# One decoder step in hybrid layers: sums of squares moved to VectorE, nine stage barriers taken out

## The chip, the cores and the metric

The kernel runs on one NeuronCore of a Trainium2 chip. The metric is the device time of one execution in microseconds (us), the median of several runs. All data is fp32; matrix products are made of three fp32r products each, as told below.

## What is computed

One step of a decoder trunk of two layers, for a prompt of 512 tokens and 8 single sample tokens, side by side: 520 columns in all, `D_MODEL` 1024. Cut to what matters here:

```python
def rmsnorm(x, g):
    return x * rsqrt(mean(x * x, axis=-1) + EPS) * g

# layer 0: sliding-window attention and mLSTM; layer 1: Mamba-2 SSD and retention
x += mixer(rmsnorm(x, norm_mix) @ w_in) @ w_out
q, k, v = rmsnorm(x, norm_xattn) @ wq, rmsnorm(mem, norm_mem) @ wk, rmsnorm(mem, norm_mem) @ wv
x += softmax(norm(q) @ norm(k).T * s) @ v @ wo              # 4 heads, 256 memory tokens
x += square(relu(rmsnorm(x, norm_ffn) @ w1)) @ w2           # FFN_DIM 4096
```

Six of these norms are over `x`: before both input projections, both cross-attentions and both MLPs.

## The kernel before

Activations stand transposed: `x` is eight chunks `c` of 128 features (partitions) by 520 tokens (columns). A **norm** is never applied to its input. `NextNorm` (L277) makes three things from each chunk of `x` as soon as it is final: on VectorE `hi = x*g` rounded to fp32r (L290) and `lo = x*g - hi` (L291), on ScalarE the square (L297), which TensorE multiplies by a matrix of ones to sum it over the partitions into PSUM banks 6 and 7, chunk after chunk (L303, two halves of 260 columns, recorded as four matmuls). When all eight are summed, ScalarE makes `rstd` from it (L310, L312). The projection that follows works on `hi` and `lo`, and VectorE multiplies its result by `rstd` when it takes it out of PSUM.

**`Gemm`** (L320) runs a list of tiles. A tile is 128 output features by 520 columns over `nk` chunks of input features (8, or 4 in the cross-attention output and the odd output projection), and three matmuls for each chunk and half: hi by hi, hi weight by lo, lo weight by hi (L356 to L358). So a tile with `nk` 8 has 48 matmuls of 260 columns, one with 4 has 24. Tiles use three pairs of PSUM banks in turn; tile n waits until tile n-3 was taken out. The weights are streamed by SyncE through a ring of two buffers (L415): load of tile n+2 once the split of tile n is done, ScalarE's rounded copy `w_hi` (L399) once the load is there and tile n is computed, GpSimd's `w_lo = w - w_hi` (L410) after it, and then TensorE may begin. VectorE takes a tile out: `out_residual` adds it to `x` (L464), `out_ssd` multiplies by a per-token factor first and then adds (L2688, L2689), `out_copy` multiplies by `rstd` (L454). A tile with `"finish": c` makes chunk c of `x` final; after it `Gemm` calls the norm's steps: VectorE `NextNorm.dve`, ScalarE `NextNorm.act`, and TensorE `NextNorm.pe` one tile later, for the last chunk right at the end, and then ScalarE `act_rstd`. `follow` and `pe_before` hang other small steps on tiles; on each engine they stand in program order, and so does every wait.

**Stages** run one after another (`plan`, L2714), and between any two `fence` (L235) makes TensorE, VectorE and ScalarE drain and wait for each other; SyncE and GpSimd stream on. There are 41 such barriers. The order around the change is:

- `Load`: 8 chunks of the input transposed on TensorE, copied to `x` by VectorE, and the first norm; then the parameter vectors; barrier; even input projection.
- Mixer of the layer, of many small stages. The last but one of the even mixer is `MlstmSample`, of the odd one `SsdSample`, each followed by a norm stage; in the odd layer `OddStored` follows (ScalarE waits for stores).
- Output projection (even: 8 tiles of `nk` 8; odd: 16 tiles of `nk` 4, two for each chunk), with the norm of the cross-attention. Its first tile issues the load of the memory tokens (1 MB, ScalarE's queue). Barrier.
- `MemLoad` (L1585): the memory tokens transposed, split into hi and lo, in layer 0 also their norm. Barrier.
- Cross projection: 4 tiles `wq`, 4 `wk`, 4 `wv`; the last eight have 256 columns. `CrossNorm` (L1866) sums the squares of each q and k head on TensorE, in banks 6 and 7 too, before tile j+2.
- The attention over the memory, then the cross output projection: 8 tiles of `nk` 4, with the norm of the MLP. Barrier; in layer 0 `OddLoads` (two DMA issues) and a barrier.
- `Ffn` (L713): 64 tiles of `nk` 8; in layer 0 its last 8 finish `x` and make the odd mixer's norm. Barrier; `ConvHistory` (12 small transposes); barrier; odd input projection.

## Time and profile before

| | |
|---|---|
| median of 3 runs | 2122.76 us (2122.05 to 2124.38) |
| span of the profiled execution | 2111.2 us |
| its own time | not listed apart from its span; the median of the runs is 11.6 us above the span |
| TensorE, matmul busy | 1857.1 us, 88% |
| VectorE busy | 845.0 us, 40% |
| ScalarE busy | 585.5 us, 28% |
| GpSimd busy | 583.7 us, 28% |
| HBM | 80 GB/s over the span |

The profile is of one execution. Busy shares are of the span; "idle before" is the time an engine stood still ahead of an instruction, and what ended it. Times of stretches are counted from the start of the span. The matmul rows show a start and a modelled end that overlaps the next, so the pace of TensorE is read from start to start. The clock is what TensorE was granted, as a share of 2.4 GHz: 1.00 is that, 0.50 is 1.2 GHz.

### The profile page before, as it was taken

How to read it: one execution, taken by the hardware profiler on the slowest of the kernel's cores; microseconds unless marked ns; L12 is line 12 of the kernel's file. 1: busy time of each engine (PE TensorE's matmuls, PEld its weight loads, DVE VectorE, ACT ScalarE, POOL GpSimd, SP SyncE). 2: the span in 40 equal slices, each digit the busy share in tenths (PEclk: the TensorE clock that was granted, in tenths of full speed). 3: DMA queues.
4: the chain of work that ended last, by engine and by line, in shares of the span. 5: the costliest groups of instructions: out<-in, count | busy, mean ns of one | idle time of the engine just before them, and what ended most of it. 6: DMA issues, size and time to landing. Idle time of an engine off the chain costs nothing. (4 is left out here: it accounts for less than half of the span.)

```text
span 2111.2 us, 31312 instructions
## 1 busy us (share of the span) xinstructions
PE 1857.1 (88%) x13432; PEld 1700.7 (81%) x13432; DVE 845.0 (40%) x1201; ACT 585.5 (28%) x1006; POOL 583.7 (28%) x260
## 2 busy tenths in 40 slices
PE   7895777996999999999899978866986899999997
PEld 6894466885599999998899956745885489999997
DVE  4445265523332121234865244668733152111211
ACT  2234202242233232322331211325232233222311
POOL 1330000250134444442343300001331034444442
PEclk9997666997999999999999975678988999999999
DMA  4221001234033333332233213113226023333332
GB/s 116 71 80 43 20 23 55 66 100 179 21 105 98 92 91 90 93 89 62 80 91 86 75 49 93 27 40 114 87 70 219 1 71 90 93 96 93 90 91 81
DMA packets 294043, 170.64 MB, mean 81 GB/s; under 512 B 18839, under 2 KB 281159, under 8 KB 293754
## 3 DMA queue, kind: packets, MB, share of 16 engines
q1 hardware_dynamic: 253016, 123.85, 21.0%
q10 hardware_dynamic: 40890, 44.79, 6.5%
q8 instruction: 107, 1.75, 0.4%
q14 instruction: 30, 0.25, 0.0%
HBM read 155.91 MB, written 13.84 MB: 80 GB/s over the span
## 5 line engine op out<-in xcount | busy, mean ns | idle before, releaser
L410 POOL TENSOR_TENSOR w_lo<-w_raw,w_hi 128x1024 fp32r<-128x1024 f32 (+2 forms) x256 | 583.5, 2279 | 1502.7 <-ACT w_hi L399 1502.6
L356 PE MATMUL banks<-xn_hi,w_hi 128*128 128x260 f32 (+1 forms) x1920 | 552.4, 288 | 17.8 <-issue 11.1
L358 PE MATMUL banks<-xn_hi,w_lo 128*128 128x260 f32 (+1 forms) x1920 | 548.4, 286 | 0.0
L357 PE MATMUL banks<-xn_lo,w_hi 128*128 128x260 f32 (+1 forms) x1920 | 546.6, 285 | 0.0
L399 ACT ACTIVATE w_hi<-w_raw 128x1024 fp32r<-128x1024 f32 (+2 forms) x256 | 252.6, 988 | 1029.8 <-PE banks L358 997.2
L356 PEld LDWEIGHTS banks<-xn_hi,w_hi 128*128 128x128 f32 (+1 forms) x1920 | 364.0, 190 | 20.7 <-issue 18.2
L357 PEld LDWEIGHTS banks<-xn_lo,w_hi 128*128 128x128 f32 (+1 forms) x1920 | 363.6, 189 | 1.6
L358 PEld LDWEIGHTS banks<-xn_hi,w_lo 128*128 128x128 f32 (+1 forms) x1920 | 363.3, 189 | 1.1
L356 PE MATMUL banks<-hid_hi,w_hi 128*128 128x260 f32 x1024 | 290.3, 284 | 0.0
L358 PE MATMUL banks<-hid_hi,w_lo 128*128 128x260 f32 x1024 | 289.4, 283 | 0.0
L357 PE MATMUL banks<-hid_lo,w_hi 128*128 128x260 f32 x1024 | 288.6, 282 | 0.0
L464 DVE TENSOR_TENSOR x<-banks,x 128x520 f32<-128x520 f32 x96 | 67.1, 699 | 345.1 <-PE banks L358 345.1
L356 PEld LDWEIGHTS banks<-hid_hi,w_hi 128*128 128x128 f32 x1024 | 192.7, 188 | 0.2
L357 PEld LDWEIGHTS banks<-hid_lo,w_hi 128*128 128x128 f32 x1024 | 192.6, 188 | 0.2
L358 PEld LDWEIGHTS banks<-hid_hi,w_lo 128*128 128x128 f32 x1024 | 192.6, 188 | 0.0
L752 DVE SCALAR_TENSOR_TENSOR relu<-banks,rstd 128x520 f32<-128x520 f32 x64 | 44.8, 700 | 291.5 <-PE banks L358 291.5
L356 PE MATMUL banks<-y_hi,w_hi 128*128 128x260 f32 x320 | 97.3, 304 | 6.3 <-DVEq L237 4.3
L357 PE MATMUL banks<-y_lo,w_hi 128*128 128x260 f32 x320 | 93.3, 292 | 0.0
L358 PE MATMUL banks<-y_hi,w_lo 128*128 128x260 f32 x320 | 93.0, 291 | 0.0
L454 DVE TENSOR_TENSOR proj<-banks,rstd 128x520 f32<-128x520 f32 (+1 forms) x49 | 34.2, 698 | 145.4 <-PE banks L358 145.3
L356 PEld LDWEIGHTS banks<-y_hi,w_hi 128*128 128x128 f32 x320 | 63.3, 198 | 14.8 <-issue 9.7
L357 PEld LDWEIGHTS banks<-y_lo,w_hi 128*128 128x128 f32 x320 | 63.4, 198 | 0.4
(487 smaller groups left out, 2635.0 us busy)
## 6 DMA issues: line engine op xcount, KB each, us to landing
w_raw<-in_ffn_w SPq DMA_DIRECT2D x128, 512.0 KB, 4.0
w_raw<-in_odd_w_in SPq DMA_DIRECT2D x36, 512.0 KB, 3.8
kc<-in_cache_mem_k ACTq DMA_DIRECT2D x16, 512.0 KB, 7.5
vc<-in_cache_mem_v ACTq DMA_DIRECT2D x16, 512.0 KB, 11.5
w_raw<-in_even_w_in SPq DMA_DIRECT2D x14, 512.0 KB, 3.8
w_raw<-in_odd_w_out SPq DMA_DIRECT2D x24, 256.0 KB, 2.7
w_raw<-in_mem_wq SPq DMA_DIRECT2D x8, 512.0 KB, 3.8
w_raw<-in_mem_wk SPq DMA_DIRECT2D x8, 512.0 KB, 3.8
```

The lines of the kernel that those rows point to most:

```text
L356: pe.matmul(out, hi[:, kk, 0:m], r, start=kk == 0, stop=False)
L357: pe.matmul(out, hi[:, kk, 0:m], q, start=False, stop=False)
L358: last = pe.matmul(out, lo[:, kk, 0:m], r, start=False, stop=kk == nk - 1)
L399: act.activation(k.w_hi[n % RING][:, 0:t["nk"], 0:t["m"]], k.w_raw[n % RING][:, 0:t["nk"], 0:t["m"]], ACT.Copy).then_inc(k.w_hi_ready.s, 1)
L410: pool.tensor_tensor(k.w_lo[n % RING][:, view[0], view[1]], k.w_raw[n % RING][:, view[0], view[1]], k.w_hi[n % RING][:, view[0], view[1]]. ...
L454: dve.tensor_tensor(d, src, r, ALU.mult).then_inc(k.tile_out.s, 1)
L464: dve.tensor_tensor(d, src, d, ALU.add).then_inc(k.tile_out.s, 1)
L752: dve.scalar_tensor_tensor(two(self.relu[h % 2][:, :]), src, 0.0, two(k.rstd[:, :]), ALU.max, ALU.mult).then_inc(k.tile_out.s, 1)
```

## The change

It has four parts.

1. ScalarE makes `hi` (activation Copy with a scale) and the square of each chunk. VectorE makes `lo` and, from the second chunk on, adds the square to `norm_acc`. TensorE multiplies `norm_acc` by the ones once (`pe_total`), at the end of the first tile of the next projection (the tile marked `normed`), and `rstd` is made after that tile; VectorE waits for it before it takes that tile out.
2. A `normed` tile waits chunk by chunk for `lo` (`pe_chunk`), and stages marked `open_end` have no barrier behind them: `Load`, both cross output projections, `Ffn` of layer 0. `OddLoads`, `ConvHistory` and `OddStored` are no stages any more: their steps hang on the first tile of `Ffn`, on the third tile of the odd input projection (bank 6), and on the start of the second `MemLoad`.
3. Output projection and cross projection become one `Gemm` behind `MemLoad`: 4 tiles `wk`, the output tiles, 4 `wq`, 4 `wv`. So `MemLoad` comes ahead of the output projection, and the load of the memory tokens is issued at the start of `MlstmSample` and of `SsdSample`. In all nine barriers fewer.
4. On VectorE the norm's steps for chunk c come after the next tile was taken out. Counters of several helpers are shared so that the semaphores suffice.

```diff
-    def __init__(self, k, gain, dst, sq):
-        self.k, self.gain, self.dst, self.sq = k, gain, dst, sq
-        self.first = k.n_squares
-        k.n_squares += DC
+    def __init__(self, k, gain, dst, last_read=None):
+        self.k, self.gain, self.dst, self.last_read = k, gain, dst, last_read
+        self.nth = k.n_norms
+        k.n_norms += 1
+        self.first, self.adds = self.nth * DC, self.nth * (DC - 1)
+
+    def act(self, act, c):
+        k, x = self.k, self.k.x[:, c, :]
+        act.activation(self.dst[0][:, c, :], x, ACT.Copy, scale=k.col(self.gain + c)).then_inc(k.norm_high.s, 1)
+        if c >= 3:
+            act.wait_ge(k.square_added.s, self.adds + c - 2)
+        square = k.norm_sq[c % 2] if c else k.norm_acc
+        act.activation(square[:, :], x, ACT.Square).then_inc(k.square_ready.s, 1)
 
     def dve(self, dve, c):
-        k, x, g = self.k, self.k.x[:, c, :], self.k.col(self.gain + c)
-        hi, lo = self.dst[0][:, c, :], self.dst[1][:, c, :]
-        k.dve_link(dve.tensor_scalar(hi, x, g, None, ALU.mult))
-        dve.scalar_tensor_tensor(lo, x, g, hi.bitcast(F32), ALU.mult, ALU.subtract)
-
-    def act(self, act, c):
-        k = self.k
-        if c >= 2:
-            act.wait_ge(k.square_summed.s, self.first + c - 1)
-        act.activation(self.sq[c % 2][:, :], k.x[:, c, :], ACT.Square).then_inc(k.square_ready.s, 1)
-
-    def pe(self, pe, c):
-        k = self.k
-        pe.wait_ge(k.square_ready.s, self.first + c + 1)
+        k = self.k
+        dve.wait_ge(k.norm_high.s, self.first + c + 1)
+        dve.scalar_tensor_tensor(self.dst[1][:, c, :], k.x[:, c, :], k.col(self.gain + c),
+                                 self.dst[0][:, c, :].bitcast(F32), ALU.mult, ALU.subtract).then_inc(k.xn_ready.s, 1)
+        if c:
+            dve.wait_ge(k.square_ready.s, self.first + c + 1)
+            if c >= 2:
+                dve.wait_ge(k.square_added.s, self.adds + c - 1)
+            dve.tensor_tensor(k.norm_acc[:, :], k.norm_acc[:, :], k.norm_sq[c % 2][:, :], ALU.add)\
+               .then_inc(k.square_added.s, 1)
+
+    def pe_chunk(self, pe, c):
+        pe.wait_ge(self.k.xn_ready.s, self.first + c + 1)
+
+    def pe_total(self, pe):
+        k = self.k
+        pe.wait_ge(k.square_added.s, self.adds + DC - 1)
+        if self.last_read:
+            sig, count = self.last_read
+            pe.wait_ge(sig.s, count)
         for b, (c0, c1) in enumerate(HALVES):
-            last = pe.matmul(k.ps[:, 6 + b, 0:HALF], k.c("ones"), self.sq[c % 2][:, c0:c1],
-                             start=c == 0, stop=c == DC - 1)
+            last = pe.matmul(k.ps[:, 6 + b, 0:HALF], k.c("ones"), k.norm_acc[:, c0:c1], start=True, stop=True)
         last.then_inc(k.square_summed.s, 1)
 
     def act_rstd(self, act):
         k = self.k
-        act.wait_ge(k.square_summed.s, self.first + DC)
+        act.wait_ge(k.square_summed.s, self.nth + 1)
         k.act_link(act.activation(two(k.rstd[:, :]), k.ps[:, 6:8, 0:HALF], ACT.Ln, scale=1.0 / D_MODEL,
                                   bias=k.c("eps")))
-        act.activation(k.rstd[:, :], k.rstd[:, :], ACT.Exp, scale=-0.5)
-
-
-def next_norm(k, name, gain, dst):
-
-    return NextNorm(k, gain, dst, [k.small(f"{name}_sq{i}", [P, TOK]) for i in range(2)])
+        act.activation(k.rstd[:, :], k.rstd[:, :], ACT.Exp, scale=-0.5).then_inc(k.rstd_done.s, 1)
+
+    def rstd_here(self, eng):
+        eng.wait_ge(self.k.rstd_done.s, self.nth + 1)
...
-            if "pe_before" in t:
-                t["pe_before"](pe)
+            for step in t.get("pe_before", ()):
+                step(pe)
...
+                if "normed" in t:
+                    t["normed"].pe_chunk(pe, kk)
...
             last.then_inc(k.tile_done.s, 1)
-            if i and "finish" in self.mine[i - 1]:
-                self.norm.pe(pe, self.mine[i - 1]["finish"])
-        if "finish" in t:
-            self.norm.pe(pe, t["finish"])
+            if "normed" in t:
+                t["normed"].pe_total(pe)
...
+        late = None
         for i, t in enumerate(self.mine):
             n = self.base + i
+            if "normed" in t and late is not None:
+                self.norm.dve(dve, late)
+                late = None
             dve.wait_ge(k.tile_done.s, n + 1)
+            if "normed" in t:
+                t["normed"].rstd_here(dve)
             w = t["halves"][0][1] - t["halves"][0][0]
             nb = len(t["halves"])
             src = ps[0:t["m"], 2 * (n % 3):2 * (n % 3) + nb, 0:w]
...
             dve.wait_ge(k.tile_out.s, n + 1)
             for step in t.get("dve_after", ()):
                 step(dve, n)
-            if "finish" in t:
-                self.norm.dve(dve, t["finish"])
+            if late is not None:
+                self.norm.dve(dve, late)
+            late = t.get("finish")
+        if late is not None:
+            self.norm.dve(dve, late)
...
                 split_high(k, act, n + RING)
+            if "normed" in t:
+                t["normed"].act_rstd(act)
             if "finish" in t:
                 act.wait_ge(k.tile_out.s, n + 1)
                 self.norm.act(act, t["finish"])
             for step in t.get("act_after", ()):
                 step(act, n)
-        if "finish" in t:
-            self.norm.act_rstd(act)
...
-            if c:
-                self.norm.pe(pe, c - 1)
-        self.norm.pe(pe, DC - 1)
         pe.wait_ge(self.late_here.s, 16 * len(self.loads))
         pe.transpose(ps[:, 5, 0:self.n0], self.rows[0][0:self.n0, :], k.c("ident", self.n0)[:, 0:self.n0])
         pe.transpose(ps[:, 5, 128:182], self.rows[1][0:54, :], k.c("ident", 54)[:, 0:54]).then_inc(self.vectors.s, 1)
+        pe.wait_ge(self.out.s, DC)
+
+    def vectors_copied(self, pe):
+        pe.wait_ge(self.out.s, DC + 1)
...
-            dve.wait_ge(self.out.s, c + 1)
-            self.norm.dve(dve, c)
+            if c:
+                self.norm.dve(dve, c - 1)
+        self.norm.dve(dve, DC - 1)
         dve.wait_ge(self.vectors.s, 1)
...
+        tiles[0]["normed"] = normed
+        super().__init__(k, tiles, NextNorm(k, V_MIX + DC, k.xn) if layer == 0 else None)
...
+        prefetch_memory(k, act, self.mtok)
...
         k.state_stores_done()
         if l:
+            k.stores_done()
...
-    tiles = [gemm_tile(k.A["mem_wq"][l], [(h * P, P)], k.xc, out_copy(k, m.q[:, h, :])) for h in range(4)]
-    for w, dst in (("mem_wk", m.k_t), ("mem_wv", m.v_t)):
-        tiles += [gemm_tile(k.A[w][l], [(h * P, P)], (m.hm_hi, m.hm_lo), out_copy(k, dst[:, h, :]), halves=[(0, MEM)])
-                  for h in range(4)]
-    CrossNorm(k, tiles, [(m.q[:, h, :], V_QN + l) for h in range(4)] + [(m.k_t[:, h, :], V_KN + l) for h in range(4)], l)
-    s.append(Gemm(k, tiles))
+    memory_tiles = lambda w, dst: [gemm_tile(k.A[w][l], [(h * P, P)], (m.hm_hi, m.hm_lo), out_copy(k, dst[:, h, :]),
+                                             halves=[(0, MEM)]) for h in range(4)]
+    tiles = memory_tiles("mem_wk", m.k_t) + out_tiles
+    first = len(tiles)
+    tiles += [gemm_tile(k.A["mem_wq"][l], [(h * P, P)], k.xc, out_copy(k, m.q[:, h, :])) for h in range(4)]
+    tiles += memory_tiles("mem_wv", m.v_t)
+    k.small.reset(2080)
+    buffers = [k.small(f"qk_{n}{l}", [P, TOK]) for n in ("sq", "rstd0", "rstd1")]
+    keys = CrossNorm(k, tiles, 0, [(m.k_t[:, h, :], V_KN + l) for h in range(4)], buffers)
+    norm = NextNorm(k, V_XATT + DC * l, k.xc, (keys.rstd_ready, keys.base + 4))
+    tiles[first]["normed"] = norm
+    CrossNorm(k, tiles, first, [(m.q[:, h, :], V_QN + l) for h in range(4)], buffers, norm)
+    s.append(Gemm(k, tiles, norm))
     s += [KvTurn(k, m, l), CrossPrompt(k, m, l), CrossSample(k, m, l)]
     w = k.A["mem_wo"][l]
-    k.small.reset()
+    norm = NextNorm(k, V_FFN + DC * l, k.xn)
     s.append(Gemm(k, [gemm_tile(w, [(c * P, P)], (k.xa_hi, k.xa_lo), out_residual(k, c), nk=4, finish=c)
-                      for c in range(DC)], next_norm(k, f"cross_out{l}", V_FFN + DC * l, k.xn)))
-    return s
...
+    history = ConvHistory(k, normed)
+    gates, conv = OddGates(k), Conv(k, history)
+    follow(tiles, 2, lambda dve, n: history.dve(dve), pe=history.pe)
...
 def plan(k):
 
     stages = [Load(k)]
+    normed = stages[0].norm
     for layer, mixer in enumerate((even_layer, odd_layer)):
-        stages += mixer(k) + cross_layer(k, layer)
+        mixed, out_tiles = mixer(k, normed)
+        crossed, normed = cross_layer(k, layer, out_tiles)
+        ffn = Ffn(k, layer, normed)
         if layer == 0:
-            stages.append(OddLoads(k))
-        stages.append(Ffn(k, layer))
+            odd_loads(k, ffn.mine)
+            ffn.open_end = True
+        normed = ffn.norm
+        stages += mixed + crossed + [ffn]
...
                 s.pe(pe)
-                k.fence(pe, "pe")
+                if not s.open_end:
+                    k.fence(pe, "pe")
```

## Rows read from the trace of the kernel before

**Rows 1.** the page: busy time, share of the span and instructions of each engine

```profile
PE 1857.1 (88%) x13432; PEld 1700.7 (81%) x13432; DVE 845.0 (40%) x1201; ACT 585.5 (28%) x1006; POOL 583.7 (28%) x260
```

**Rows 2.** windows: bounds, length, busy by engine (instructions), clock, DMA share, GB/s

```profile
349.89:405.67 55.78, 54.94 (x416) 53.28 (x416) 30.92 (x24) 12.70 (x17) 18.44 (x8) 0.97 0.29 86
416.40:470.66 54.26, 51.90 (x408) 49.71 (x408) 10.79 (x19) 22.59 (x35) 25.69 (x11) 1.00 0.30 88
562.28:593.71 31.43, 30.62 (x224) 28.99 (x224) 24.17 (x24) 10.81 (x16) 11.79 (x8) 1.00 0.29 81
596.61:605.20 8.59, 8.59 (x51) 8.59 (x52) 0.03 (x1) 0.00 (x0) 0.00 (x0) 0.69 0.55 201
978.26:989.00 10.74, 10.74 (x68) 8.24 (x69) 1.98 (x3) 1.15 (x2) 0.85 (x1) 0.72 0.05 16
1469.82:1530.67 60.85, 55.74 (x416) 52.61 (x416) 44.45 (x47) 15.27 (x24) 23.27 (x16) 1.00 0.31 96
1690.98:1723.88 32.90, 32.09 (x224) 30.46 (x224) 24.04 (x24) 10.69 (x16) 11.89 (x8) 0.95 0.28 78
1725.51:1733.00 7.49, 7.49 (x52) 7.49 (x53) 0.07 (x1) 0.01 (x1) 0.00 (x0) 0.81 0.27 70
1730.00:1800.00 70.00, 70.00 (x588) 70.00 (x587) 16.09 (x23) 25.39 (x36) 30.56 (x12) 1.00 0.30 84
```

**Rows 3.** timeline, TensorE, one sum of squares between two tiles; start, us, instruction

```profile
362.80 1.04 PE L303 MATMUL banks<-even_out_sq,const 128*128 128x260 f32 x4
...
363.80 0.28 PE L357 MATMUL banks<-y_lo,w_hi 128*128 128x260 f32 x1
```

**Rows 4.** waits: total us, times, longest; even, then odd output projection

```profile
PE banks L303 <- ACT even_out_sq L297: 0.8, 1, 0.8
...
PE banks L303 <- ACT odd_out_sq L297: 5.1, 8, 2.3
```

**Rows 5.** timeline, TensorE: first matmul after six of the barriers [idle before it]

```profile
32.58 0.40 PE L356 MATMUL banks<-xn_hi,w_hi 128*36 128x260 f32 x1 [1.36 <-ACTq L237]
407.29 0.57 PE L1624 MATMUL banks<-const,mem_tok 128*128 128x128 f32 x2 [1.67 <-ACTq L237]
596.61 0.56 PE L356 MATMUL banks<-xn_hi,w_hi 128*128 128x260 f32 x1 [2.90 <-ACTq L237]
976.62 0.33 PE L679 MATMUL banks<-const,conv_old 24*128 24x24 f32 x3 [1.67 <-ACTq L237]
978.26 0.38 PE L356 MATMUL banks<-xn_hi,w_hi 128*16 128x260 f32 x1 [0.74 <-DVEq L237]
1725.51 0.56 PE L356 MATMUL banks<-xn_hi,w_hi 128*128 128x260 f32 x1 [1.63 <-DVEq L237]
```

**Rows 6.** weight split by shape, whole kernel: count, busy us, mean ns, idle before

```profile
L399 ACT ACTIVATE w_hi<-w_raw 128x512 fp32r<-128x512 f32 x40 | 25.1, 628 | 142.4 <-PE banks L358 134.2 <-DMA w_raw<-in_mem_wo 8.1
...
L410 POOL TENSOR_TENSOR w_lo<-w_raw,w_hi 128x1024 fp32r<-128x1024 f32 x214 | 530.2, 2478 | 978.9 <-ACT w_hi L399 978.8
L410 POOL TENSOR_TENSOR w_lo<-w_raw,w_hi 128x512 fp32r<-128x512 f32 x40 | 52.0, 1301 | 508.6 <-ACT w_hi L399 508.6
```

**Rows 7.** DMA issues: KB each, median us from issue to landing

```profile
w_raw<-in_ffn_w SPq DMA_DIRECT2D x128, 512.0 KB, 4.0
...
w_raw<-in_mem_wo SPq DMA_DIRECT2D x16, 256.0 KB, 2.7
```

**Rows 8.** VectorE by line, duration ns least/median/most

```profile
L2689 DVE TENSOR_TENSOR x<-x,odd_out_t x16: 699/1447/2678, 1473.8 to 1528.0; 128x520 f32<-128x520 f32 x16
...
L291 DVE SCALAR_TENSOR_TENSOR xc_lo<-x,vcol,xc_hi x16: 758/1768/2883, 358.6 to 1531.3; 128x520 fp32r<-128x520 f32 x16
...
L464 DVE TENSOR_TENSOR x<-banks,x x96: 684/700/701, 357.3 to 2094.6; 128x520 f32<-128x520 f32 x96
```

**Rows 9.** timeline, odd output projection: an add of VectorE and GpSimd beside it

```profile
1491.32 1.76 DVE L2689 TENSOR_TENSOR x<-x,odd_out_t 128x520 f32<-128x520 f32 x1
...
1491.23 1.30 POOL L410 TENSOR_TENSOR w_lo<-w_raw,w_hi 128x512 fp32r<-128x512 f32 x1 [2.92 <-ACT w_hi L399]
```

More of the change, by code:

```diff
@@ L465, in out_residual, with follow @@
     return emit
-def follow(tiles, i, dve=None, act=None):
-    for key, step in (("dve_after", dve), ("act_after", act)):
+def follow(tiles, i, dve=None, act=None, pe=None):
+    for key, step in (("dve_after", dve), ("act_after", act), ("pe_before", pe)):
         if step:
@@ L678, in pe @@
                 rows, n = src.shape
-                last = pe.transpose(k.ps[0:n, 4 + i % 4, c0:c0 + rows], src, self.ident(src, rows))
+                last = pe.transpose(k.ps[0:n, self.bank + i % 4, c0:c0 + rows], src, self.ident(src, rows))
             last.then_inc(self.done.s, 1)
@@ L756, in dve @@
             dve.wait_ge(k.tile_out.s, n + 1)
-            if "finish" in t:
-                self.norm.dve(dve, t["finish"])
+            if late is not None:
+                self.norm.dve(dve, late)
+            late = t.get("finish")
             if pending is not None:
@@ L761, in dve @@
             pending = t.get("hidden")
+        if late is not None:
+            self.norm.dve(dve, late)
     def act(self, act):
@@ L769, in act @@
                 split_high(k, act, n + RING)
+            if "normed" in t:
+                t["normed"].act_rstd(act)
+            for step in t.get("act_after", ()):
+                step(act, n)
             if "hidden" in t:
@@ L913, in even_projection @@
         tiles.append(gemm_tile(w, [(c * P, P)], xn, out_copy(k, k.proj[:, c, :], scale)))
+    follow(tiles, 2, pe=k.load.vectors_copied)
     gates = EvenGates(k)
@@ L1589, in __init__ @@
         super().__init__(k)
[L1590 removed]
+        k.small.reset()
         self.mtok = k.mtok
@@ L2187, in ret_turn, with spread_decays @@
     return Turn(k, "ret_turn", items)
-def spread_decays(k, pairs, banks):
-    return Beside(k, f"ssd_decays{pairs[0]}", [(k.pair(j, 16, (0, SEQ), k.ecum[:, 0:SEQ]), lambda act, bank, j=j:
+def spread_decays(k, which, pairs, banks):
+    return Beside(k, which, [(k.pair(j, 16, (0, SEQ), k.ecum[:, 0:SEQ]), lambda act, bank, j=j:
                                                 act.activation(k.ec[:, j, 0:SEQ], bank[:, :], ACT.Copy))
@@ L2765, in program @@
         k.n_row_norms, k.n_logs = 0, 0
+        k.rope_signals, k.n_ropes = (k.counter("rotated"), k.counter("rotation_free")), 0
+        k.beside_signals = [(k.counter(f"beside{i}_full"), k.counter(f"beside{i}_free")) for i in range(2)]
+        k.n_beside = [0, 0]
         k.row_norm_signals = [k.counter(f"row_norm_{n}") for n in ("squared", "summed", "rstd", "normed")]
```

190 lines of the change are left out of this document (101 added, 89 removed).

## Prediction, made before the changed kernel was run

> **What bounds it now.** Start with the page: TensorE is busy for 88% of the span, every other engine for 40% or less [rows 1]. Then cut the span into stages. In the long MLP stretch TensorE starts 588 matmuls in 70.00 us, at the full 2.4 GHz and without idle time [rows 2]: 0.119 us each, so 5.71 us for a tile with `nk` 8 and 2.86 us for one with 4. Nothing there touches a norm, and the change leaves it alone. Compare the output projections with that pace. The even one takes 55.78 us for 8 tiles (45.7 us at that pace), the first cross output projection 31.43 for 22.9, the odd one 60.85 for 45.7 [rows 2]. The difference is work of TensorE that is not a product with weights, and waits. The timeline shows the first: from the start of a sum of squares to the second matmul after it is 1.00 us where one matmul would take 0.12, so a pair of 260-column sums costs 0.88 us, I take 0.9 [rows 3]; fp32 sums run slower than fp32r products. Last, look at what TensorE does behind barriers: it stands for 0.74 to 2.90 us [rows 5], and then often runs at 1.2 GHz for a while. The first MLP tile took 8.59 us instead of 5.71, at a granted clock of 0.69; 68 matmuls after the barrier into the odd projection took 10.74 us instead of 8.1; 52 in the second MLP 7.49 instead of 6.2 [rows 2]. TensorE is the path in all these stages, so what it is spared counts nearly in full.
>
> **The change, stage by stage.** Six norms of 8 sum pairs become six pairs, one for each. I keep 0.9 us for each of these, on TensorE's path, since it comes right behind the first tile of the next projection.
>
> *Load.* Here VectorE and not TensorE sets the pace, and it trades `hi` for an add, which is no gain. What goes is the end: the last pair, the barrier's 1.36 us of idleness [rows 5], and the wait for chunk 7's `lo`, which now lies beside the first seven chunks of the first tile. I take 3.2 us, less 0.9 for the sum: **-2.3**.
>
> *Even output and cross projection.* 55.78 becomes 45.7 + 0.9 = 46.6, -9.2. In it are the 0.8 us wait for the last square [rows 4] and a start at 1.2 GHz (granted mean 0.97). One barrier goes, -1.7 [rows 5]. `MemLoad` now comes behind small mixer stages and may begin at the lower clock, +0.5. The cross projection holds 54.26 us with 51.90 of matmuls [rows 2]: its 256-column tiles (2.8 us) outrun the weights, where a pair of tiles needs a 512 KB load of 4.0 us and a split of 2.5 us on GpSimd besides ScalarE's copy [rows 6, 7]. Cut into two groups of four, each group has two filled buffers ahead of it; -1.0. **-11.4**.
>
> *First cross output into MLP.* 31.43 becomes 22.9 + 0.9, but now the first MLP tile needs a 512 KB weight tile after 2.86 us tiles. Worked from the tile two before it: split done 2.0 us after that tile (0.63 + 1.30), load 4.0, copy 1.1 (just under twice 0.63), split 2.5, makes 9.6, and TensorE is ready at 8.6: +1.0. So 24.8, -6.6. The gap of 2.90 us goes, and with it, I think, the slow first tile, 8.59 - 5.71 = 2.9. **-12.4**. The two DMA issues of `OddLoads` now stand on ScalarE's queue in the first MLP tile, some 0.8 us in which ScalarE has nothing due; they wait for nothing.
>
> *MLP into odd projection.* 8 pairs 7.2, the last wait 0.8 (as in [rows 4]), gaps 1.67 and 0.74 [rows 5], slow start 2.6; back comes the one sum, 0.9. The 12 transposes stay on TensorE, moved. **-12.1**.
>
> *Odd output and cross projection.* 60.85 includes 5.1 us in which the sums wait for squares [rows 4], because here VectorE is late. It takes two tiles out for each chunk, with an add of two SBUF operands each time, and these adds are stretched: 0.70 us at best, 1.45 in the median, 2.68 at most [rows 8]. [Rows 9] show why: the add that began at 1491.32 ended at 1493.08, half a microsecond after GpSimd's split that had begun at 1491.23. VectorE's work for a chunk is now 0.7 x 5 + 0.76 = 4.3 us unstretched, beside 2.6 us of GpSimd in 5.7 us. The part that both need, 2.9 + 2.6 = 5.5 us, fits only just, and ScalarE's next weight copy stands behind its wait for the tile that is taken out. I take 0.5 us for each chunk lost, 4 us (bounds 0 and 8: none, and a split held back for 1 us for each chunk). So 45.7 + 0.9 + 4 + 1.0 (the step to 512 KB weights) = 51.6, -9.25. Barriers: -1.7, and -0.7 for `OddStored`'s, by the 0.74 of one with little ahead of it [rows 5]. Weights -1.0. **-12.6**.
>
> *Second cross output into MLP.* 32.90 becomes 22.9 + 0.9 + 1.0 and its own start at 1.2 GHz, 1.6 by its granted mean of 0.95 [rows 2]: 26.4, -6.5; gap -1.6 [rows 5]; slow start -1.3. **-9.4**.
>
> *What costs nothing.* 42 adds of 0.70 us on VectorE and 48 copies of some 0.63 on ScalarE lie in stages where both are half idle; uncovered they would be 60 us, as much as the whole gain. Chunk 7 is the tight one: from the end of the last tile, taking it out 0.7, `lo` and add of chunk 6 with GpSimd's 2.5 us split between, `lo` of chunk 7: some 5 us, and TensorE asks for it after 7/8 of a tile, 5.0 us. `rstd` now comes after the first tile (copy 1.1; Ln and Exp 1.3, by the 0.63 of a 512-column copy [rows 6]), so that tile is taken out 2.5 us late, which three bank pairs cover. The memory loads move to stages where ScalarE's queue is empty, and compete there for 5 us; the stores that `MemLoad` waits for were issued a stage earlier. 0, at worst +2.
>
> Sum: 2.3 + 11.4 + 12.4 + 12.1 + 12.6 + 9.4 = 60.2 us. From the span of 2111.2 that makes 2051.0; what lies around a span, 11.6 us to the median, I leave as it is: 2122.76 - 60.2 = 2062.6, say **2063 us**.
>
> **Rivals.** *Port collisions* (0.15). Every new add, and every `lo`, reads two SBUF operands, and such instructions and GpSimd's split exclude each other: `lo` took 0.76 us at best and 2.88 at most, while taking out a tile from PSUM never went over 0.701 in 96 times [rows 8]. If VectorE comes first, the split waits, and behind it TensorE. In the 32 tiles of 2.86 us the split is done about 0.8 us before it is needed, so a `lo` of 0.76 ahead of it is still covered and an add of 0.70 behind that is not: 0.7 x 32 = 22 us lost, 4 of it already counted: 2080. Against it: GpSimd starts 0.6 us after a tile ends, while VectorE still reads PSUM. The Trainium skill, page "SBUF — State Buffer", section "Who interferes with whom", says that whichever of the two starts first keeps the shared ports for its whole instruction and the other blocks fully; by that rule the change adds 42 instructions that can hold up the split. The stretched durations here agree with it.
>
> *The clock is not regained* (0.12). The slow starts at 596.61, 978.26 and 1725.51 follow gaps of 2.90, 0.74 behind 1.67, and 1.63 us, but 416.40 ran at 1.00 at once [rows 2]. If waits for weights or `lo` keep the low clock, 2.9 + 2.6 + 1.3 and the 1.7 of the even output projection come back: 2071.
>
> *The barrier lives on as a wait* (0.10). If chunk 7's `lo` is 1.5 to 2 us late at five joints, that takes 7 to 10 us back: 2070 to 2072.
>
> *Slower* (0.03). Place: the two output projections behind `MemLoad`. They now start from a stage at half clock with GpSimd-bound short tiles ahead. If TensorE's idle bits in these kept the clock at 1.2 GHz through both, their 91 us of tiles would take up to twice as long: +91 us against a gain of 60, 2154. It decides only if two thirds of both stages stay slow. Against: the even output projection started from such a stage too, and its granted mean of 0.97 over 55.78 us [rows 2] leaves some 3 us at half clock.
>
> **How the numbers follow.** My forecast has 0.60. Its own range is 2056 (no loss in the odd stage, memory loads free) to 2070. Port collisions and the two waits reach 2080; 2055 to 2081 holds about 8 in 10. A measurement of this kernel can tell about 0.2%, 4 us, from no change; that is only between forecast and slower, and hardly likely: faster 0.96, same 0.01, slower 0.03.
>
> **What would show it.** In the changed profile: 6 groups of 4 sums where 48 were; no idle time over 0.5 us between the last output tile and the first tile of the next projection, apart from about 1 us for weights at the two MLPs; the first MLP tile in 5.8 us; VectorE adds of 0.70 us at best with a tail to 2.5. Wrong would be: TensorE waiting for `w_lo` in the 2.86 us tiles (port), waiting for `lo` at the eighth chunk (barrier lives on), a granted clock under 0.9 behind the joints, or a stage not touched here that is longer than before.

## The result and the profile after

The changed kernel takes **2065.43 us** (median of 4 runs, 2060.29 to 2066.09), the kernel before in the same series 2122.41 (2121.48 to 2124.38): ratio 0.9729, 95% interval 0.9706 to 0.9753. The forecast was 2063, in a range of 2055 to 2081, and "faster".

The page of the changed kernel, to be read against [rows 1]:

```profile
span 2064.3 us, 30998 instructions
PE 1817.6 (88%) x13264; PEld 1668.7 (81%) x13264; DVE 834.6 (40%) x1195; ACT 615.8 (30%) x1054; POOL 589.6 (29%) x260
```

TensorE has 168 matmuls and 39.5 us of work less, ScalarE 30 us more, and the share of TensorE is as before: what went was its own work and its idle time together. By line: busy us, mean ns of one, and idle time before; then the durations of VectorE's adds in ns, least, median and most:

```profile
L325 PE MATMUL banks<-norm_acc,const 128*128 128x260 f32 x24 | 6.2, 382 | 0.0
L312 DVE TENSOR_TENSOR norm_acc<-norm_acc,norm_sq 128x520 f32<-128x520 f32 x42 | 63.1, 1502 | 0.0
...
L297 ACT ACTIVATE xn_hi<-x,vcol 128x520 fp32r<-128x520 f32 x32 | 23.2, 725 | 8.9 <-DVE x L643 4.9 <-DVE x L493 3.5
```

```profile
L312 DVE TENSOR_TENSOR norm_acc<-norm_acc,norm_sq x42: 686/690/2907, 18.7 to 1683.6; 128x520 f32<-128x520 f32 x42
```

Six groups of four recorded matmuls stand where 48 groups were, and the adds are the foreseen 0.69 us at best, with a long tail. The windows that answer to [rows 2] (bounds, length, busy by engine, clock, DMA share, GB/s) in order of time:

```profile
373.42:420.50 47.08, 47.08 (x389) 47.03 (x390) 26.89 (x22) 17.02 (x26) 20.34 (x8) 1.00 0.33 96
583.68:590.20 6.52, 6.52 (x53) 6.43 (x53) 5.15 (x6) 2.03 (x4) 2.41 (x1) 1.00 0.58 163
945.00:965.00 20.00, 19.88 (x165) 18.21 (x163) 9.94 (x13) 6.93 (x12) 5.49 (x3) 1.00 0.39 106
1453.26:1461.00 7.74, 7.74 (x47) 7.74 (x48) 0.42 (x1) 1.37 (x2) 1.05 (x1) 0.67 0.00 0
1468.74:1517.51 48.77, 47.88 (x387) 46.86 (x386) 41.40 (x47) 20.60 (x35) 21.82 (x16) 1.00 0.33 98
1519.57:1527.00 7.43, 7.43 (x49) 7.43 (x50) 4.58 (x5) 1.26 (x2) 2.69 (x1) 0.77 0.48 143
```

The even output tiles take 47 us where 55.78 stood and never pause (the one sum that is left no longer lies among them, but behind the first `wq` tile). The first MLP tile with its sum takes 6.5 us at a granted clock of 1.00, where the old one without a sum took 8.59. The join of MLP and odd projection, at 945 to 965, has next to no idle time and a granted clock of 1.00. The odd output tiles take 48.8 where 60.85 stood. Two rows are less good: in layer 1 the first `wk` tiles and the first `wq` tile run at a granted 0.67 and 0.77, so partly at 1.2 GHz. The joints in the timeline of TensorE (start, us, [idle before it]), to be read against [rows 5]:

```profile
583.68 0.36 PE L377 MATMUL banks<-xn_hi,w_hi 128*128 128x260 f32 x1 [1.20 <-issue]
...
1519.57 0.37 PE L377 MATMUL banks<-xc_hi,w_hi 128*128 128x260 f32 x1 [1.78 <-ACT w_hi L427]
...
1679.01 0.36 PE L377 MATMUL banks<-xn_hi,w_hi 128*128 128x260 f32 x1 [1.21 <-issue]
```

Two idle times of 1.2 us ahead of the MLPs, and a new one of 1.78 us ahead of `wq` in layer 1.

Stage by stage in us, each length from the first TensorE matmul of one stage to that of the next. The second pair of traces comes from the first two experiments below, which are the same two kernels again.

| part | forecast | first pair | second pair |
|---|---|---|---|
| Load and even input projection | -2.3 | 163.1 to 159.6, -3.6 | 162.3 to 160.1, -2.2 |
| even output, `MemLoad`, cross projection | -11.4 | 121.62 to 112.63, -9.0 | 125.69 to 115.08, -10.6 |
| first cross output, MLP, odd projection | -24.5 | 649.2 to 627.1, -22.1 | 650.6 to 627.1, -23.5 |
| odd output, `MemLoad`, cross projection | -12.6 | 128.62 to 116.62, -12.0 | 129.43 to 116.05, -13.4 |
| second cross output, MLP | -9.4 | 404.5 to 394.3, -10.2 | 404.4 to 395.8, -8.6 |
| sum of the changed parts | -60.2 | -56.8 | -58.2 |
| all that was not touched | 0 | +9.9 | -1.8 |
| span | | 2111.2 to 2064.3, -46.9 | 2121.7 to 2061.7, -60.0 |

The changed parts agree between the pairs to within 2 us each; the untouched ones move by 10 in all. That was the first thing to settle.

### The profile page after: what moved, and what is told of

Same layout as the page of the kernel before. It is cut to its first block, busy times and chain, and to the rows that moved or that the text cites. A ratio compares the mean times of both kernels' runs of the same rounds, so it can differ in the third digit from the quotient of the medians.

```text
span 2064.3 us, 30998 instructions
## 1 busy us (share of the span) xinstructions
PE 1817.6 (88%) x13264; PEld 1668.7 (81%) x13264; DVE 834.6 (40%) x1195; ACT 615.8 (30%) x1054; POOL 589.6 (29%) x260
## 4 chain that ended last, share of the span: by engine, by line
PE 78%; DVE 11%; ACT 4%; ACTq 2%; issue 2%; DMA 1%; SPq 0%; POOL 0%; DVEq 0%
PE banks L377 21%; PE banks L379 20%; PE banks L378 20%; ACTq L1808 2%; PE banks L1859 2%; PE banks L864 1%; PE banks L1870 1%; ACT w_hi L427 1%; PE banks L1848 1%; PE banks L2384 1%; PE banks L2505 1%; ACT xa_s L1798 1%; PE banks L682 1%; PE banks L2464 1%; PE banks L1758 1%
## 5 line engine op out<-in xcount | busy, mean ns | idle before, releaser
L438 POOL TENSOR_TENSOR w_lo<-w_raw,w_hi 128x1024 fp32r<-128x1024 f32 (+2 forms) x256 | 589.4, 2303 | 1449.8 <-ACT w_hi L427 1449.7
L312 DVE TENSOR_TENSOR norm_acc<-norm_acc,norm_sq 128x520 f32<-128x520 f32 x42 | 63.1, 1502 | 0.0
```

The source lines that it names most:

```text
L312: dve.tensor_tensor(k.norm_acc[:, :], k.norm_acc[:, :], k.norm_sq[c % 2][:, :], ALU.add)\
L438: pool.tensor_tensor(k.w_lo[n % RING][:, view[0], view[1]], k.w_raw[n % RING][:, view[0], view[1]], k.w_hi[n % RING][:, view[0], view[1]]. ...
```

## Experiments

The first four ran on one chip between the same 13 runs of the kernel before (median 2117.11), the next four on a second chip between 7 (2118.49), then two on a third between 11 (2116.14), and two on the second again between 9 (2117.34). Ratios are against these; the square brackets hold 95% intervals. The changed kernel ran beside the first four (2065.77) and beside the last two (2068.32), not beside the four in the middle. So each of these is compared with both, and a difference of 3 us between kernels from different groups says little.

### Both kernels once more

> The kernel before, unchanged, to get a second trace of it. The trace I read had a span of 2111.2 us, the runs a median of 2122 us; the changed kernel's span lies only 1.8 us below its time. Theory 'phase': the stages that the change does not touch (even mixer, attention over the memory, odd mixer) run at either granted clock by chance of phase, and differ between two traces of one kernel by some us each; then this trace has a span near 2120 us and its unchanged stages are longer than those I read by 5 to 10 us in all. Rival 'cost': the change itself made those stages longer by 10 us (shared counters, memory load moved, other neighbours); then this trace repeats the lengths that I read: CrossSample of layer 0 in 42.9 us at a clock of 1.00, RetSample's stretch in 60.7 us.

> The changed kernel, unchanged, timed beside the others: 0.973 of the kernel before. Its trace shows which of its stages vary from run to run: theory 'phase' expects CrossSample of layer 0 (45.8 us at 0.93 in the first trace) and the retention stage (64.2 us at 0.65) to move by 1 to 3 us in either direction; rival 'cost' expects them to stay.

Measured: before 2120.68 (10 runs, 2111.32 to 2125.31), ratio 1.0011 [0.9991, 1.0032]; after 2065.77 (4 runs, 2063.47 to 2069.05), ratio 0.9759 [0.973, 0.9787]. `CrossSample` of layer 0, which neither kernel changes, in four windows (columns as above): the kernel before in its first and second trace, then the changed one in its first and second. Under the last two stands a retention stage of the same trace, untouched too.

```profile
518.80:562.28 43.48, 37.40 (x163) 17.09 (x164) 5.37 (x13) 9.24 (x18) 0.00 (x0) 1.00 0.00 0
```

```profile
519.80:566.50 46.70, 40.62 (x164) 18.31 (x164) 5.37 (x13) 9.24 (x18) 0.00 (x0) 0.93 0.00 0
```

```profile
511.00:557.38 46.38, 40.30 (x164) 18.57 (x164) 5.37 (x13) 9.24 (x18) 0.00 (x0) 0.92 0.00 1
1184.50:1214.70 30.20, 22.77 (x128) 18.49 (x129) 12.88 (x25) 4.19 (x9) 0.00 (x0) 0.66 0.31 84
```

```profile
511.40:557.95 46.55, 40.46 (x164) 18.27 (x164) 5.37 (x13) 9.24 (x18) 0.00 (x0) 0.93 0.00 1
1185.10:1212.00 26.90, 19.63 (x128) 16.20 (x129) 12.73 (x25) 4.17 (x9) 0.00 (x0) 0.75 0.28 75
```

VectorE and ScalarE work for 5.37 and 9.24 us in all four windows of `CrossSample`; only TensorE's clock and with it the length differ, 43.5 us at 1.00 and 46.4 to 46.7 at 0.92 or 0.93. The retention stage took 30.20 us at 0.66 and 26.90 at 0.75, in one and the same kernel. So what such a stage takes goes with the clock that this execution got there, and 3 us of difference in one such stage say nothing of a change. The rival 'cost' is not excluded everywhere: from the first matmul of `RetSample` to the first of the norm stage behind it the kernel before took 62.7 us in both traces, the changed one 65.8, 62.6 and, in a third trace, 65.8. It can be as short as before, but three traces do not show whether the change makes the long case more frequent. The runs also show what the first trace of the kernel before was: in all of them the time lies 1.7 to 2.0 us above the span (2066.06 above 2064.3 for the changed kernel), so the execution with span 2111.2 was one of about 2113 us, at the low end of the kernel's spread, and not one of 2122 with 11.6 us around it.

### The barriers put back

```diff
-                if not s.open_end:
+                if True:
```

> The changed kernel with a barrier behind every stage again, so that the four open ends (Load, both cross output projections, first MLP) close. Theory: each barrier costs its idle time, 1.4 to 1.7 us, and the late steps of the last chunk, some 2 us more, and the clock falls to half behind it, 2.9 + 2.6 + 1.3 us: 2065 + 6 + 6 + 7 = 2084 us (ratio to before 0.982). Rival 'the barrier lives on as a wait': the waits for lo, weights and rstd take its place, and this is slower by under 5 us.

Measured: 2090.29 (2087.84 to 2096.3), ratio 0.9877 [0.9847, 0.9908]; **+24.5 us** over the changed kernel beside it, where 19 were expected. The trace is of the longest of the four runs. The timeline of TensorE behind the four barriers put back (Load, first MLP, odd projection, second MLP), and that of GpSimd and VectorE ahead of the second of them:

```profile
31.05 0.40 PE L377 MATMUL banks<-xn_hi,w_hi 128*36 128x260 f32 x1 [4.96 <-DVEq L242]
...
593.54 0.56 PE L377 MATMUL banks<-xn_hi,w_hi 128*128 128x260 f32 x1 [6.47 <-DVEq L242]
...
970.55 0.38 PE L377 MATMUL banks<-xn_hi,w_hi 128*16 128x260 f32 x1 [5.72 <-DVEq L242]
...
1706.74 0.56 PE L377 MATMUL banks<-xn_hi,w_hi 128*128 128x260 f32 x1 [6.76 <-DVEq L242]
```

```profile
585.43 2.75 POOL L438 TENSOR_TENSOR w_lo<-w_raw,w_hi 128x1024 fp32r<-128x1024 f32 x1 [2.05 <-ACT w_hi L427]
585.87 2.87 DVE L312 TENSOR_TENSOR norm_acc<-norm_acc,norm_sq 128x520 f32<-128x520 f32 x1
...
588.66 0.68 DVE L493 TENSOR_TENSOR x<-banks,x 128x520 f32<-128x520 f32 x1
...
589.38 2.12 DVE L306 SCALAR_TENSOR_TENSOR xn_lo<-x,vcol,xn_hi 128x520 fp32r<-128x520 f32 x1
591.43 0.69 DVE L312 TENSOR_TENSOR norm_acc<-norm_acc,norm_sq 128x520 f32<-128x520 f32 x1
592.04 0.75 DVE L306 SCALAR_TENSOR_TENSOR xn_lo<-x,vcol,xn_hi 128x520 fp32r<-128x520 f32 x1
592.71 0.68 DVE L312 TENSOR_TENSOR norm_acc<-norm_acc,norm_sq 128x520 f32<-128x520 f32 x1
```

TensorE stands 5 to 7 us at these barriers, where the kernel before stood 1.36, 2.90, 1.67 with 0.74, and 1.63 [rows 5]. The second fence says what it waits for: VectorE is one chunk behind, its add begins beside a split of GpSimd and takes 2.87 us instead of 0.69, and six instructions have to end before the barrier opens at 593.4. The changed kernel has the same chain (its add at 581.27 also takes 2.87 us), but TensorE starts at 583.68 on chunk 0 and runs ahead of it. Behind the barrier TensorE is at the lower clock again for part of the time, in the window of the first MLP tile:

```profile
593.50:603.00 9.50, 9.46 (x53) 9.38 (x54) 0.00 (x0) 0.57 (x1) 0.00 (x0) 0.68 0.11 32
```

The rival "the barrier lives on as a wait" falls: in the changed kernel the open ends are worth 24.5 us. By this trace most of it is idle time (23.9 us at the four joints, against 1.96, 1.20, 0 and 1.21 in the changed kernel); the rest is clock.

### The sums taken out of the kernel before

In the kernel before, only the last chunk's square is summed on TensorE:

```diff
-        pe.wait_ge(k.square_ready.s, self.first + c + 1)
+        if c < DC - 1:
+            return
+        pe.wait_ge(k.square_ready.s, DC * (self.first + 1))
```

> The kernel before with only the last of the eight sums of squares of each norm left on TensorE (the squares of seven chunks are left out of the norm), all barriers and the order as before. Theory: 42 pairs less at 0.88 us, 35 of them in the five Gemm stages, and the 4 to 5 us in which the odd output projection waited for squares: 35 us less, 2087 us (ratio 0.983); Load, where VectorE sets the pace, gives nothing. Rival: the pairs were partly cover for the weight split (TensorE then waits for w_lo in the tiles of 2.86 us), and only 20 us go: 2102 us.

Measured: 2094.63 (2090.71 to 2094.88), ratio 0.9889 [0.9862, 0.9917], 22.5 us under the kernel before beside it, where 35 were expected. Two waits tell part of why. The timeline at the last sum of the cross output and of the odd output projection, first in the kernel before, then without the sums:

```profile
592.57 1.14 PE L303 MATMUL banks<-cross_out_sq,const 128*128 128x260 f32 x4 [0.81 <-ACT cross_out_sq L297]
...
1529.45 1.22 PE L303 MATMUL banks<-odd_out_sq,const 128*128 128x260 f32 x4 [2.27 <-ACT odd_out_sq L297]
```

```profile
587.83 2.10 PE L305 MATMUL banks<-cross_out_sq,const 128*128 128x260 f32 x4 [2.79 <-ACT cross_out_sq L297]
...
1511.80 2.10 PE L305 MATMUL banks<-odd_out_sq,const 128*128 128x260 f32 x4 [5.33 <-ACT odd_out_sq L297]
```

Without the sums of the chunks before, TensorE reaches the last one earlier and stands there for VectorE and ScalarE; and the four recorded matmuls themselves, behind that idle time, take 2.10 us instead of 1.14 and 1.22, at a granted clock of 0.51 and 0.50. Part of the sums had covered the tail of the last chunk. That the sums would pay more with open ends is not shown: the next experiment puts 35 pairs into the kernel with open ends, and they cost 20 to 22.5 us there, no more than the 22.5 that the 42 pairs, 35 of them outside Load, gave here.

The four kernels of this chip in order: 2117.1 before, 2094.6 without the sums, 2090.3 with all of the change but the four open ends (two output projections merged with their cross projections, five barriers fewer, but 42 adds more), 2065.8 with them. The steps are not single changes: the second also moves `hi` to ScalarE and the one sum behind the next tile. No run opens the ends of the kernel before, so how the 51 us divide between sums and barriers is not shown.

### The sums given back to the changed kernel

35 pairs of matmuls like the old sums (fp32, 260 columns, banks 6 and 7, a constant as data), five norms by seven chunks, behind the tile after each finished chunk. Nothing of the result is changed.

```diff
+            if i and self.mine[i - 1].get("finish", DC) < DC - 1:
+                self.norm.pe_extra(pe, self.mine[i - 1]["finish"])
```

> The changed kernel with a pair of 260-column fp32 matmuls (on constants, result unused) put back on TensorE behind each of the first seven finishing tiles, in the five Gemm stages: 35 pairs, with no wait of their own. Nothing else of the sums returns. Theory: TensorE is the path there, a pair costs its 0.88 us: 35 x 0.88 = 31 us, less 2 to 3 us where TensorE waited for weights at the joints anyway: 2065.5 + 28 = 2094 us. Rival, from the run with one sum (24 us less instead of 35): the pairs are in part cover for other work also in the changed kernel: +20 us, 2085 us.

Measured: 2088.29 (2087.24 to 2089.98), ratio 0.9858 [0.9825, 0.9891]; 22.5 us over 2065.77 and 20.0 over the 2068.32 of the changed kernel on the same chip, 0.57 to 0.64 a pair. The stage that is VectorE's, odd output and cross projection, grew by 2.7 us for 7 pairs, and the joint into the first MLP by 4.2; there the pairs fill the wait for weights. From the first MLP matmul to the end of the odd projection, where nothing else is late, 7 pairs cost 6.0 us (606.8 against 600.8), 0.86 each: a pair costs its 0.88 us only in such a place.

### The adds left out, and doubled

```diff
-        if c:
+        if c == DC - 1:
```

> The changed kernel with 36 of the 42 adds on VectorE left out (only the last chunk's square is added, so the sum of squares lacks chunks 1 to 6); ScalarE, TensorE and barriers as they are. Forecast's term: 4 us lost in the odd output projection to VectorE and GpSimd, so 2061 us. What the trace of the changed kernel now suggests: TensorE's waits inside that stage add up to 1.5 us, and the rest hides, so 2064 us. Rival 'port collisions': the adds hold up the weight split everywhere, and 10 us or more go.

```diff
+            k.dve_link(dve.tensor_tensor(k.norm_acc[:, :], k.norm_acc[:, :], k.norm_sq[c % 2][:, :], ALU.add))
             dve.tensor_tensor(k.norm_acc[:, :], k.norm_acc[:, :], k.norm_sq[c % 2][:, :], ALU.add)\
```

> The changed kernel with each add of a square done twice (squares of chunks 1 to 7 count twice): 42 more VectorE instructions of 0.69 us with two SBUF operands. Theory: no room is left where tiles take 2.86 us: in the odd output projection the part that VectorE and GpSimd share grows from 5.5 to 6.2 us for each chunk of 5.7 us, in the cross output projections from 2.8 to 3.5 us of 2.86 us; 4 us lost in the first, 3 to 5 us in each of the other two, nothing in the stages with 5.7 us tiles: 2065.5 + 12 = 2078 us. Rival: two bank pairs of slack take it up and it costs under 3 us.

Measured: without 36 of 42 adds 2058.50 (2057.22 to 2059.13), ratio 0.9715 [0.9688, 0.9742], 7 us under the changed kernel's 2065.77 and 10 under the 2068.32 of the same chip; with 42 more 2081.07 (2076.57 to 2085.85), ratio 0.9823 [0.9789, 0.9857], 15 and 13 us over it. That is 0.2 to 0.27 us for an add of the change, and 0.30 to 0.36 for one more behind it (which also waits for the one it repeats). The first kernel leaves the squares of six chunks out of the norm, the second counts seven twice. Nearest to one place is Load: the first projection matmul stood at 25.3 us without adds, at 27.9 in the changed kernel, at 31.7 with twice as many. The timeline of VectorE in Load of the changed kernel:

```profile
25.15 0.68 DVE L642 COPY x<-banks 128x512 f32<-128x512 f32 x1
25.75 0.15 DVE L643 COPY x<-banks 128x8 f32<-128x8 f32 x1
25.83 0.75 DVE L306 SCALAR_TENSOR_TENSOR xn_lo<-x,vcol,xn_hi 128x520 fp32r<-128x520 f32 x1
26.50 0.69 DVE L312 TENSOR_TENSOR norm_acc<-norm_acc,norm_sq 128x520 f32<-128x520 f32 x1
27.11 0.68 DVE L642 COPY x<-banks 128x512 f32<-128x512 f32 x1
```

A step of 1.96 us for a chunk without a gap between instructions: here the add is on the path. Elsewhere MLP with odd projection lost 1.9 us to the adds and the odd output stage 1.3 or 0.7, by which trace one takes. All this is far from the 22 us that the rival had.

### Short tiles spread out

The 256-column tiles were taken to be the ones that outran the weights. Here each `wk` tile stands ahead of an output tile of its own (two in layer 1), and `wv` tiles between `wq` tiles.

```diff
-    tiles = memory_tiles("mem_wk", m.k_t) + out_tiles
+    for h in range(4):
+        tiles += [ks[h]] + out_tiles[h * step:(h + 1) * step]
+    tiles += out_tiles[4 * step:]
```

> The changed kernel with another order in the two joined Gemms: the four wk tiles each followed by one chunk's output tiles, and the wv tiles set between the wq tiles (q0 v0 q1 v1 q2 q3 v2 v3). Same work. Theory: TensorE waits some 4.3 us (layer 0) and 5.4 us (layer 1) in these, mostly for the weights of short tiles that follow each other; spaced out, 3 and 2 us of these go: 2060.5 us. Rival: the load of 512 KB between loads of 256 KB moves the wait and does not remove it: 2065.5 us.

Measured: 2069.42 (2068.04 to 2071.86), ratio 0.9769 [0.9741, 0.9797]: no gain; it lies 3.7 us over 2065.77 and 1.1 over the 2068.32 of the same chip. Layer 0 took 112.41 us (112.63 and 115.08 in the changed kernel's traces), layer 1 119.81 (116.62 and 116.05). In layer 1 TensorE's starts show gaps of 0.6 to 1.5 us at five places around the `wk` tiles, and one of 2.6 us ahead of `wq`. That fits the rival, that the wait only moves: where the output tiles are 2.86 us long there is no slack in which a 512 KB weight tile could be made up for. The reason was not tested by itself.

### Load's adds behind Load

What the adds cost in Load can be had without leaving them out. With a buffer for each square, VectorE makes all eight `lo` first and the seven adds behind them, beside the first projection tile:

```diff
-        if c:
+        if self.nth == 0:
+            if c == DC - 1:
+                for i in range(1, DC):
+                    dve.wait_ge(k.square_ready.s, i + 1)
...
+                    dve.tensor_tensor(k.norm_acc[:, :], k.norm_acc[:, :], k.load_sq[i - 1][:, :], ALU.add)\
+                       .then_inc(k.square_added.s, 1)
+        elif c:
```

> The changed kernel, but in Load VectorE makes all eight lo first and adds the seven squares behind them, from buffers of their own. The cost-in-the-cadence theory: the adds lengthen Load's step for each chunk, and leaving them out there brought the first projection 2.65 us forward; behind the last lo they are 7 x 0.69 = 4.8 us of VectorE beside a first tile of 5.7 us or more, so nothing waits for them. Expected 2.6 us less than the changed kernel, some 2063, with the first projection matmul at about 25.3 us after the start instead of 27.9. The rival, that the 4.8 us come back as a wait of TensorE for the total at the end of the first tile, or of the third tile for a bank: the first matmul is as early, but the stage behind it longer by as much, 2065 to 2067.

The second kernel also puts the four `wk` tiles of layer 0, and of that layer alone, each ahead of one output tile.

> The kernel with Load's adds behind the lo, and in layer 0 alone the four wk tiles of 256 columns each ahead of one of the first four output tiles (the wq and wv tiles as in the changed kernel). Full interleaving in both layers left layer 0 as it was or 2.7 us shorter and made layer 1 3.5 us longer. If the small tiles starve for weights only when they stand together, this takes the waits of about 1 us each out of the wk group of layer 0 without the new ones of layer 1: 1 to 2.5 us less than the kernel with the late adds alone, 2061. Rival: the waits only move to the 48-matmul tiles behind each small one, as in layer 1: the same as the late adds alone, 2063.

Measured: 2060.07 (2057.34 to 2064.99), ratio 0.973 [0.9708, 0.9753], and 2061.47 (2053.52 to 2064.77), ratio 0.9732 [0.9707, 0.9758]. The first projection matmul came at 24.97 and 24.81 us, and the stage behind it took 131.8 and 131.6 us, against 131.7 before the edit: nothing came back as a wait. The timeline of VectorE in the first of them:

```profile
24.17 0.67 DVE L653 COPY x<-banks 128x512 f32<-128x512 f32 x1
24.77 0.15 DVE L654 COPY x<-banks 128x8 f32<-128x8 f32 x1
24.85 1.63 DVE L308 SCALAR_TENSOR_TENSOR xn_lo<-x,vcol,xn_hi 128x520 fp32r<-128x520 f32 x2
26.39 5.52 DVE L316 TENSOR_TENSOR norm_acc<-norm_acc,load_sq 128x520 f32<-128x520 f32 x7
```

The seven adds stand in one block of 5.5 us and end at 31.9; TensorE comes to the total at 32.42. The `wk` tiles of layer 0 gave nothing that can be told (112.10 us). Since the changed kernel had not run beside these, one more pair did:

> The changed kernel as it is, timed on the same chip and between the same runs as the kernel with Load's adds behind the lo, because the two were so far only compared through the kernel before, whose own time moves by 10 us. 2061 to 2066 expected. If its median lies 2 to 4 us above the other's, the 2.9 us seen at the first projection matmul reach the end of the kernel; if it is the same within 1 us, they are lost in what the clock does behind.

> The kernel with Load's adds behind the lo, as it is, beside the changed kernel in the same call: 2 to 4 us less than that, by the 2.9 us that its first projection matmul came earlier; rival: no difference within 1 us.

Measured: the changed kernel 2068.32 (2059.46 to 2070.33), ratio 0.9759 [0.9733, 0.9785]; with the late adds 2060.08 (2052.14 to 2069.52), ratio 0.9716 [0.9691, 0.9741]. The medians differ by 8 us, more than the edit explains: in the two traces of this pair the first projection matmul again came 3.1 us earlier (24.96 and 28.07), but the spans were 2067.7 and 2068.5, since the clock in the stages behind differed. Over all their runs the medians are 2066.1 (12 runs) and 2060.1 (10 runs). So 3 us are shown at their place; how much of the other 3 to 5 is chance stays open. It is the fastest version that leaves nothing out of the result.

## Why the prediction was right

The forecast said -60, the changed parts gave -57 and -58 in two pairs of traces, and the runs 57, 51 and 49 us (2122.4 to 2065.4, 2117.1 to 2065.8, 2117.3 to 2068.3). That the time itself came within 2.4 us has some luck in it: the 2122.76 it was taken from is high among the 54 runs of the kernel before (median 2118.9), and the two later series gained 9 and 11 us less than forecast. The mechanism held: TensorE is the path, and it was spared sums, idle time at barriers and time at the lower clock. By its steps:

- **"0.9 us a pair."** Right where TensorE has nothing to wait for: from the first MLP matmul to the end of the odd projection the forecast's terms make 14.1 us, and the traces have 614.9 to 600.8 and 614.8 to 600.9. Taken over all stages the sums alone are cheaper, 0.57 to 0.64 a pair given back, and 22.5 us for the 42 pairs taken out of the kernel before, because some lie where TensorE would have waited.
- **"The gap goes", at four joints.** Right for what the kernel before lost there, some 8 us of idleness and 7 of slow starts. What the prediction did not see is that barriers kept in the changed kernel would be dearer (5 to 7 us of idleness each), since VectorE now has adds to finish before they open. Open ends and adds belong together; with barriers the change was worth 27 us, without them 51. These 24.5 us are a price in the changed kernel and no term of the forecast's sum, so they neither confirm nor correct it.
- **"With it, I think, the slow first tile."** Right at both MLPs and at the odd projection, where the granted clock is 1.00. Missed is the first cross output projection: it was put at 22.9 us and took 25.1, since its first 7.62 us ran at a granted 0.79. In the first trace of before the same place had 1.00, in the second 0.77. The rival "clock not regained" came true in one small part that had not been listed: behind the 1.78 us ahead of `wq` in layer 1, 49 matmuls took 7.43 us, 1.6 more than at 0.119 each, and the first `wk` tile of that layer, behind `MemLoad`, took 7.74 us for 47, 2.3 over the 5.4 that this many take in layer 0. The wait alone does not settle the clock. In the second trace of the changed kernel the same 1.78 us stood ahead of the same tile, and TensorE went on at 1.00, with 59 matmuls in the same time:

```profile
1517.36 0.36 PE L377 MATMUL banks<-xc_hi,w_hi 128*128 128x260 f32 x1 [1.78 <-ACT w_hi L427]
```

```profile
1517.36:1524.80 7.44, 7.44 (x59) 7.33 (x60) 4.61 (x5) 2.68 (x4) 3.01 (x2) 1.00 0.48 143
```

- **Load, -2.3.** -3.6 and -2.2. But the step "it trades `hi` for an add, which is no gain" was kept as neither gain nor loss, and it was a loss that could be avoided: 2.65 us, by the kernel without adds and by the one with late adds.
- **Even output projection, 46.6.** 46.8, from its first matmul at 373.42 to the first of `wq` at 420.24, but without the sum that the 46.6 includes; so 1.1 more than the 45.7 of the pace. What failed besides is the -1.0 for weights in the groups of four: around the `wk` group TensorE waited 0.67 and 0.67 us for weights and 0.94 for ScalarE's square of a key head, and the stage gave 9.0 to 10.6 instead of 11.4.
- **MLP weights, +1.0.** 1.20 and 1.21 us.
- **Odd output projection, 4 us lost to VectorE and GpSimd.** Rather 2: 48.8 us where the pace makes 45.7, and the even stage, with no wait at all, also has 1.1 us over its pace. In exchange the step to 512 KB weights, taken as 1.0, was 1.78 us, with the lower clock behind it in two of three traces (0.77, 1.00, 0.77).
- **Port collisions.** As a mechanism they are there, as a bound they are not. The add at 585.87 began 0.44 us after a split of GpSimd and ended 0.56 us after it, 2.87 us for 0.69. The Trainium skill, page "SBUF — State Buffer", section "Who interferes with whom", has it that the later of two such instructions is blocked until the earlier has ended, and this row agrees. But it was mostly VectorE that waited: its 42 adds took 63.1 us instead of 29, while GpSimd's large splits went from a mean of 2478 ns [rows 6] to 2496 and the small ones from 1301 to 1354 (below). Behind VectorE stand three pairs of banks, which can take up its delay. The adds cost 7 to 10 us in all, 2.65 of these in Load, where GpSimd is not the cause. The prediction had put 22 us on it in the rival and 4 in the forecast. GpSimd's splits in the changed kernel by line and shape (count, busy us, mean ns, idle before):

```profile
L438 POOL TENSOR_TENSOR w_lo<-w_raw,w_hi 128x1024 fp32r<-128x1024 f32 x214 | 534.0, 2496 | 964.1 <-ACT w_hi L427 964.1
L438 POOL TENSOR_TENSOR w_lo<-w_raw,w_hi 128x512 fp32r<-128x512 f32 x40 | 54.2, 1354 | 471.8 <-ACT w_hi L427 471.7
```

- **"11.6 us around a span, left as it is."** Wrong in its reading and harmless in its use, because the gain was taken from the median of the runs. It is 1.8 us; the rest was a short execution. Had the sum been taken from the span alone and 1.8 added, the forecast would have been 2053.
- **"Its own range is 2056."** The two terms named for it do not reach that: 2062.6 less the 4 us of the odd stage is 2058.6, and the memory loads were already at 0. In the same way chunk 7's steps add up to 5.4 us (0.7, 0.76, 0.7, 2.5, 0.76), not "some 5", against the 5.0 after which TensorE asks; none of the three traces of the changed kernel has a wait for it there.

Of the rivals only parts were seen: some us of clock, 7 to 10 us of adds instead of 22, and no wait in place of a barrier. That does not make the chances (0.60 for the forecast, 0.37 for the three together) too timid: the gains of 51 and 49 us in the later series, taken from 2122.76, would be 2071 and 2074.

## What to carry to other kernels

A barrier here cost what the slowest engine still had to do when the fastest arrived, and some clock behind it. The change with the four barriers left in gave 27 us, without them 51. So when work moves from the bounding engine to an idle one, open the barrier in the same step, and let the consumer wait chunk by chunk. The price of a part depends on what else is in place: measure it by undoing that part in the final version too. Where another engine sets the pace for a moment, as in Load, put the moved work behind that moment. And take a second trace of the same kernel before reading a stage that differs by 3 us.

## What was not expected of the hardware

- **The clock of half-busy stages differs from execution to execution.** The same `CrossSample` ran at 1.00 in 43.5 us and at 0.93 in 46.7, the same retention stage at 0.75 in 26.9 and at 0.66 in 30.2. The kernel before spread from 2110.7 to 2127.3 us over its 54 runs.
- **The same wait left different clocks.** Behind 1.20 us at 583.68 TensorE went on at 1.00. Behind 1.78 us ahead of `wq` in layer 1 it had 0.77 in the first trace and 1.00 in the second, in one and the same kernel. Behind the 6.47 us at a barrier it had 0.68.
- **Extra work on VectorE seems to grow dearer with its amount.** 36 adds cost 7 to 10 us, 42 more another 13 to 15. The repeated adds also wait for the ones they repeat, so the amount alone is not shown to be the cause.
